# A two-layer decoder trunk on eight cores: the order of an attention slot, bf16 copies of the weights in DRAM, and a logarithm that stays in its PSUM bank

## What is computed (the reference, cut)

```python
for layer in range(2):
    xn = rmsnorm(h, mix_norm_g[layer])
    if layer == 0:
        p = xn @ ab_w_in                      # 1024 -> 2048
        a_out = pool_mixer(a, pool_w, scale)  # trailing means over 2, 4, 8, 16 tokens
        b_out = gate_b * short_conv(gate_c * xb, conv_w, conv_b)
        mix = concat(a_out, b_out) @ ab_w_out
    else:
        p = xn @ cd_w_in                      # 1024 -> 2560
        c_out = spatial_gating(gelu(u), gelu(v), ...)
        d_out = stick_breaking_attention(q, k, v)   # 8 heads of 64, causal
        mix = concat(c_out, d_out) @ cd_w_out
    h = h + mix
    hn = rmsnorm(h, mlp_norm_g[layer])
    h = h + square(relu(hn @ w1)) @ w2        # 1024 -> 4096 -> 1024
return rmsnorm(h, final_norm_g)
# attention: weights = sigmoid(z) * exp(sum over s<j<t of log(1 - sigmoid(z_j)))
```

## Time and profile before

| what | us |
|---|---|
| median of 3 runs | 3147.63 (3145.16 to 3204.56) |
| the profiled execution, device time | 3141.67 |
| its span (first to last instruction, slowest core) | 3140.0 |
| spans of the 8 cores | 3131.6 to 3140.0 |
| TensorE busy | 3028.5 |
| VectorE, ScalarE, GpSimd busy | 1546.5, 1648.8, 928.9 |

### The profile page before, as it was taken

The page is one execution under the profiler, slowest core; times in us unless marked ns, Lnnn a source line. Parts: engine busy times, 40 slices in busy tenths (PEclk is TensorE's granted clock), DMA queues, the critical chain, the costliest instruction groups (busy, mean ns, idle before and its releaser), DMA issues.

```text
span 3140.0 us, 47346 instructions; the slowest of 8 cores (3131.6 to 3140.0 us)
## 1 busy us (share of the span) xinstructions
PE 3028.5 (96%) x14493; PEld 1386.1 (44%) x14493; DVE 1546.5 (49%) x2691; ACT 1648.8 (53%) x3105; POOL 928.9 (30%) x1289
## 2 busy tenths in 40 slices
PE   7999989999989998999999999999999999998998
PEld 3444434444444443444444444444444444443443
DVE  5534556444544447654444664454544464445444
ACT  3312456555466666766664454555666776653212
POOL 5311654111631125411137421144111231115111
PEclk9999999999999999999999999999999999999999
DMA  8455734544754444444456344367343373348543
GB/s 168 68 81 83 167 62 72 73 66 78 150 105 62 63 88 124 82 59 62 62 117 127 58 67 70 61 136 143 56 59 57 65 170 56 57 64 193 78 73 79
DMA packets 159669, 279.46 MB, mean 89 GB/s; under 512 B 16576, under 2 KB 33088, under 8 KB 159424
## 3 DMA queue, kind: packets, MB, share of 16 engines
q0 software_dynamic: 103824, 189.05, 41.2%
q1 hardware_dynamic: 54448, 85.28, 8.8%
q10 hardware_dynamic: 1152, 2.10, 0.2%
HBM read 423.43 MB, written 41.94 MB: 148 GB/s over the span
## 4 chain that ended last, share of the span: by engine, by line
PE 86%; DVE 4%; POOL 3%; DMA 3%; issue 2%; ACT 2%; SPq 1%; DVEq 0%; ACTq 0%; POOLq 0%
PE ps L415 70%; PE ps L961 4%; PE ps L1004 4%; PE ps L989 4%; PE ps L992 3%; POOL acc L525 1%; DMA mix<-mixd 1%; DVE xn L552 1%; DMA mixd<-mix 1%; SPq L469 1%; POOL st L687 0%; PE ps L532 0%; DMA hT<-xT 0%; PE ps L964 0%; POOL wring L394 0%
## 5 line engine op out<-in xcount | busy, mean ns | idle before, releaser
L415 PE MATMUL ps<-xn,wring 128*128 128x512 bf16 x5888 | 1354.0, 381 | 6.7 <-DVE st L666 3.5
L415 PE MATMUL ps<-mix,wring 128*128 128x512 bf16 x5120 | 1166.7, 380 | 14.5 <-DMA mix<-mixd 9.9
L394 POOL DMA_DIRECT2D wring<-wblk x720 | 387.8, 541 | 1712.0 <-PE ps L415 858.8
L415 PEld LDWEIGHTS ps<-xn,wring 128*128 128x128 bf16 x5888 | 574.1, 98 | 681.2 <-issue 26.0
L584 DVE TENSOR_TENSOR hT<-ps,hT 128x512 f32<-128x512 f32 x640 | 442.2, 691 | 705.9 <-PE ps L415 655.5
L415 PEld LDWEIGHTS ps<-mix,wring 128*128 128x128 bf16 x5120 | 499.3, 98 | 601.2 <-issue 20.2
L618 DVE TENSOR_TENSOR mix<-st 128x512 bf16<-128x512 f32 x512 | 358.0, 700 | 612.3 <-ACT st L616 607.7
L616 ACT ACTIVATE st<-ps 128x512 f32<-128x512 f32 x512 | 305.3, 597 | 543.0 <-PE ps L415 538.8
L968 ACT ACTIVATE E<-ps 128x512 f32<-128x512 f32 (+3 forms) x640 | 338.9, 530 | 350.1 <-PE ps L961 194.9
L970 ACT ACTIVATE Lp<-E 128x512 bf16<-128x512 f32 (+3 forms) x640 | 362.0, 566 | 61.6 <-ACT E L968 3.7
L525 POOL TENSOR_TENSOR acc<-acc,sq 128x512 f32<-128x512 f32 x222 | 283.4, 1277 | 290.5 <-ACT sq L519 281.4
(11 more groups left out here) (71 smaller groups left out, 1267.5 us busy)
## 6 DMA issues: line engine op xcount, KB each, us to landing
wring<-wblk POOLq DMA_DIRECT2D x720, 256.0 KB, 5.0
hsp<-hT SPq DMA_DIRECT2D x64, 256.0 KB, 4.2
hT<-hsp SPq DMA_DIRECT2D x64, 256.0 KB, 12.9
hT<-xT SPq DMA_DIRECT2D x56, 256.0 KB, 10.7
oT<-st SPq DMA_DIRECT2D x56, 256.0 KB, 10.8
mix<-mixd SPq DMA_DIRECT2D x8, 1024.0 KB, 9.7
mixd<-mix SPq DMA_DIRECT2D x8, 512.0 KB, 7.1
mixd<-qT SPq DMA_DIRECT2D x32, 128.0 KB, 4.0
```

The source lines that it names most:

```text
L394: (lambda slot, b: (lambda e: e.dma_start(out=self.wring[:, slot, :], in_=self.wblk[b])))(slot, b),
L415: self.S.op("pe", (lambda l, r, i: (lambda pe: pe.matmul(ap, lhsT=l, rhs=r, start=(i == 0), stop=(i == n - 1))))(l, r, i), reads=lts, writ ...
```

## The change

Three parts, independent of one another:

- In `prefetch`, the first use of a block still goes through GpSimd's casting DMA. The block is noted in a list, and the `take` that claims it issues a copy from SyncE's queue, from the ring slot to a new internal DRAM tensor `wbf` of bf16 blocks. The three later uses of each block are plain bf16 loads from `wbf`, issued from SyncE's queue. So there are 180 casting loads, 180 copies and 540 plain loads. A slot's next load also waits for the slot's copy.
- The norm's Ln writes its PSUM bank in place, and Exp reads and writes that bank. The two `ms` tiles go.
- In the attention's `slot`, `st2(n-2)` and `st3(n-3)` are issued ahead of `st1(n)`. The conditions and the stages themselves are as before.

```diff
+        self.wbf = nc.dram_tensor("wbf", [NBLK, 128, 1024], BF16, kind="Internal").ap()
+        self.L_wbf = [None] * NBLK
...
+    def copy_out(self, gb, b, slot):
+        self.S.op("sp", lambda e: e.dma_start(out=self.wbf[b], in_=self.wring[:, slot, :]),
+                  reads=[self.L_ring[slot]], writes=[self.L_wbf[b]], dma_key=("wb", slot))
+
     def prefetch(self, upto=None, after=()):
...
-            self.S.op("pool",
-                      (lambda slot, b: (lambda e: e.dma_start(out=self.wring[:, slot, :], in_=self.wblk[b])))(slot, b),
-                      reads=after, writes=[self.L_ring[slot]], dma_key=("ring", slot))
+            L = self.L_ring[slot]
+            if self.L_wbf[b] is None:
+                self.S.op("pool", (lambda slot, b: (lambda e: e.dma_start(out=self.wring[:, slot, :], in_=self.wblk[b])))(slot, b),
+                          reads=after, writes=[L], dma_key=("ring", slot))
+                self.L_wbf[b] = LT("wbf")
+                self.copies.append((gb, b, slot))
+            else:
+                self.S.op("sp", (lambda slot, b: (lambda e: e.dma_start(out=self.wring[:, slot, :], in_=self.wbf[b])))(slot, b),
+                          reads=[self.L_wbf[b]], writes=[L], dma_key=("hring", slot))
             self.blk_next += 1
...
         assert self.blk_use <= self.blk_next
+        for x in [x for x in self.copies if x[0] < self.blk_use]:
+            self.copies.remove(x)
+            self.copy_out(*x)
         return [(gb + i) % RING for i in range(n)]
...
-            S.op("act", lambda e: e.activation(out=ms[:], in_=nb, func=AF.Ln, scale=1.0 / D, bias=self.cf[:, 60:61]),
-                 reads=[self.L_bank[bi], self.L_cf], writes=[L_ms])
-            S.op("act", lambda e: e.activation(out=nb, in_=ms[:], func=AF.Exp, scale=-0.5),
-                 reads=[L_ms], writes=[self.L_bank[bi]])
+            L_nb = self.L_bank[bi]
+            S.op("act", lambda e: e.activation(out=nb, in_=nb, func=AF.Ln, scale=1.0 / D, bias=self.cf[:, 60:61]),
+                 reads=[L_nb, self.L_cf], writes=[L_nb])
+            S.op("act", lambda e: e.activation(out=nb, in_=nb, func=AF.Exp, scale=-0.5), reads=[L_nb], writes=[L_nb])
...
                 carry(n - 1)
-            if n < N:
-                st1(n)
             if 0 <= n - 2 < N:
                 st2(n - 2)
             if 0 <= n - 3 < N:
                 st3(n - 3)
+            if n < N:
+                st1(n)
```

More of the change, by code:

```diff
@@ L260, in __init__ @@
         self.blk_done = 0
+        self.copies = []
         self.bank_rr = 0
@@ L264, in __init__ @@
         self.nms = 0
-        self.nmt = 0
         self.nvb = 0
@@ L299, in _alloc @@
         self.wmt = sb("wmt", [128, 512], BF16)
-        self.ms = [sb("ms%d" % i, [128, 512], F32) for i in range(2)]
         self.sq = [sb("sq%d" % i, [128, 512], F32) for i in range(2)]
@@ L324, in _alloc @@
         self.L_cf, self.L_cg, self.L_cb, self.L_wmt, self.L_ones = (LT(x) for x in ("cf", "cg", "cb", "wmt", "ones"))
-        self.L_ms = [LT("ms%d" % i) for i in range(2)]
         self.L_sq = [LT("sq%d" % i) for i in range(2)]
@@ L536, in last @@
                 return
-            m = self.nmt % 2
-            self.nmt += 1
-            ms, L_ms = self.ms[m], self.L_ms[m]
-            S.op("act", lambda e: e.activation(out=ms[:], in_=nb, func=AF.Ln, scale=1.0 / D, bias=self.cf[:, 60:61]),
-                 reads=[self.L_bank[bi], self.L_cf], writes=[L_ms])
-            S.op("act", lambda e: e.activation(out=nb, in_=ms[:], func=AF.Exp, scale=-0.5),
-                 reads=[L_ms], writes=[self.L_bank[bi]])
+            L_nb = self.L_bank[bi]
+            S.op("act", lambda e: e.activation(out=nb, in_=nb, func=AF.Ln, scale=1.0 / D, bias=self.cf[:, 60:61]),
+                 reads=[L_nb, self.L_cf], writes=[L_nb])
+            S.op("act", lambda e: e.activation(out=nb, in_=nb, func=AF.Exp, scale=-0.5), reads=[L_nb], writes=[L_nb])
             for k in range(8):
-                self.later(1 + k // rate, (lambda k: (lambda: apply(k, nb, self.L_bank[bi])))(k), key)
+                self.later(1 + k // rate, (lambda k: (lambda: apply(k, nb, L_nb)))(k), key)
         def apply(k, ms, L_ms):
```

## The result

The changed kernel runs in 0.9877 of the time before (95% interval 0.9854 to 0.9899): 38.7 us less of 3146.4. Three of its five executions took 3105.6 to 3107.9 us; in the two others the cores of one die were granted a lower clock, and these, which the median of 3131.8 us on record holds, are left out of the comparison. The profiled execution's span is 3104.1 us against 3140.0. The sign and the range of the prediction held; the forecast of 21 us less was 18 us short, and the gain lies a little outside the 8 to 35 us that it allowed for its own mechanism.

A forecast was written before the change was run, and what follows sets the result against it. TensorE, busy 3028.5 of 3140.0 us, was taken to bound the kernel, leaving 111.5 us idle to win. Terms: 15 + 7 + 9 - 8 - 2 = 21 us won, so a median of 3127 us, range 3098 to 3162.

The forecast's parts named there:

- The slot's order: Attention slot: Exp first on ScalarE, scores last on TensorE, 1.8 us more slack; net 15 us won.
- 23 of the 26 us: Scores matmul L961 waiting for Exp L996: nearly all 24 waits would go; a quarter taken back, 18 us won.
- 3 us worse: Scores now stand behind waits of L1004 and L989: 0.2 us of matmul behind each of 14, 3 us lost.
- GpSimd's relief: 540 loads leave GpSimd, ending stalls mainly at the end of the first p1: 7 us won, bounds 0 and 10.
- 2.6 + 1.7 us here, 1 us at the same place of sequence B: End of first p1: 2.6 us of TensorE waits and 1.7 us of lowered clock won, 1 us in sequence B.
- DMA time: Start of last segment: plain loads shorten the DMA burst, ending the mix tile's wait; 9 us won, bounds -3 and 14.
- keeping 9 against the smaller figure: Last segment: queues served by turns would give some 3 us; 9 kept, as the long burst gave casts their turns.
- The copies at the start: First take: copies queue behind the constants and hold GpSimd's next load some 9 us; 8 us lost, bounds 0 and 15.
- SyncE's order: p1: loads of x stand behind waiting weight loads, some 11 us later but still hidden; 2 us charged.
- more than expected: Rival: short waits form one loop, so L1004's and L989's shrink too and clock stays up; 3107 us, chance 0.10.
- The gain doesn't arrive: Rival: ScalarE itself is short in late windows, so the slot's wait only moves; about 3145 us, chance 0.20.
- slower: Rival: SyncE's one queue; first copy holds GpSimd, weights' waits delay x and h; 3173 us, chance 0.12.

The follow-up runs named there:

- experiment 3: The changed kernel with the 540 plain bf16 loads issued from GpSimd's queue in place of SyncE's; span 3119.5 us, ratio 0.9924 to the kernel before.

## Why the prediction was right or wrong

1. *The slot's order: 15 us forecast, 22.7 measured.* The mechanism held: the Exp of L996 was the last of three and is now the first, and the scores' wait is gone. The size of what it could win was wrong. I took "23 of the 26 us" from the list of waits. That list counts idle time of an engine, and a matmul of 512 columns is shown for 0.38 us while the next one starts 0.216 us after it. So 0.165 us of every wait lies under the modelled end of the matmul before it. In the kernel before, steady part of attention A1:

```profile
1401.03 1.89 PE L415 MATMUL ps<-mix,wring 128*128 128x512 bf16 x8
1402.76 0.38 PE L961 MATMUL ps<-qp,kT 128*128 128x512 bf16 x1
...
1418.86 1.89 PE L415 MATMUL ps<-xn,wring 128*128 128x512 bf16 x8
1420.85 0.38 PE L961 MATMUL ps<-qp,kT 128*128 128x512 bf16 x1
```

From group to scores it is 1.73 us the first time and 1.99 the second: 0.26 us lost, of which the engine looks idle for 0.10. Counted from start to start over the whole trace, the scores behind a dense group lost 45.4 us in 132 waits, not 26.0 in 24. "3 us worse" for the waits of L1004 and L989 was the other wrong size. The same count for every order, each matmul's start against the one before it plus that one's shown time less 0.165 us (medians of the cores whose matmul records are complete):

| kernel, TensorE's order | scores | first suffix sum | Wt times V | freed | span less, measured |
|---|---|---|---|---|---|
| before: scores, sums, Wt times V | 45.7 | 8.6 | 20.5 | | |
| slot's order alone: sums, Wt times V, scores | 2.7 | 10.5 | 35.6 | 26 | 22.7 |
| ScalarE's order alone | 9.1 | 10.7 | 23.2 | 32 | 32.7 |
| changed kernel: sums, Wt times V, scores | 2.7 | 7.8 | 31.7 | | |
| changed, sums, scores, Wt times V | 7.0 | 7.4 | 19.7 | 8 | 7.7 |
| changed, scores, sums, Wt times V | 8.1 | 6.0 | 20.4 | 8 | 10.7 |

So the slot's edit frees 43 us at the scores and gives 15 back at Wt times V and 2 at the sums, where I had 3 us for both. What the count says is freed and what the spans show agree to about 3 us in all four pairs.

2. *GpSimd's relief: 7 us forecast with bounds of 0 and 10, 17.3 measured.* The places were right: the seven loads of rows 6 and the same place of sequence B. The step that failed is "2.6 + 1.7 us here, 1 us at the same place of sequence B". The stall reaches further: the late norm delays the first attention slots behind it, with a wait of L989 for L952 of 2.7 us and another fall of the clock (0.83 and 0.82 from 430 to 440 us in the kernel before, 1.00 at the same place, 435 to 450 us, in the changed one). The runs show 10.5 us for sequence A and 4.9 us for B.

3. *DMA time: 9 us forecast for the last segment, 4 to 6 measured there.* The changed kernel gains 4.2 us on the kernel before from place 2500 to 2525, and 5.7 from place 2500 to the end (medians of the cores). The step that failed is "That removes the 6.56 us [...] with the residual's 4.6 us [...] left as they are": it is the other way round. The waits for h (1.5 to 3.4 us in six of the eight cores before) and the 2.0 us for GpSimd's sum ahead of them are gone: no core of the changed kernel has one over 1.5 us there. TensorE meets the mix tile sooner and waits 6.3 to 9.2 us for it (4.5 to 7.9 before), and the clock still falls, to 0.54 and 0.50. The reason that I gave for keeping 9 against the smaller figure fails with it. By the rule of the Trainium skill ("DMA: Bandwidth & Descriptors", section "SWDGE vs HWDGE vs iDMA") that queues of the two kinds are served by turns, the gain there would have been near 3 us; the traces have 4 to 6, nearer to that than to 9. No run isolates the turns: with the mix tile on the other queue it landed after 13.8 in place of 15.0 us (medians) and the run was 3.6 us shorter. A further 6 us or so came ahead of the last segment change, which I had at nothing; where it arises isn't shown.

4. *The copies at the start: 8 us forecast with bounds of 0 and 15, 12.5 measured (14.4 on the slowest cores).* The chain was as described, to about 1 us: the constants ahead, the first copy late, GpSimd's load waiting 10.15 us (some 9 forecast). The part that failed is that TensorE would feel "about 6 us": it felt all of it, in one wait of 13.4 to 14.5 us on the eight cores, since GpSimd was in the chain of the first mixer with no slack and waited a second time, for slot 1's copy. The granted clock was 0.50 from 50 to 60 us, inside the wait, and 0.64 in the next 5 us.

5. *SyncE's order: 2 us forecast.* Outside the mix tile, TensorE's list for the slowest core has no wait over 1.3 us for x, h or a weight load behind the first x, so the cover held; no run tests the term by itself. The wait of SyncE for casting loads ahead of their copies (316.7 us in 98) is hidden.

6. *The logarithm: 0, measured as no change that can be told.* 24 and 20 ns less per instruction in the run with this edit alone.

The sum by measured terms closes if it is taken along one chain of kernels (before, the slot's order alone, the run of experiment 3, the changed kernel), by the medians of the eight cores: slot 22.4, GpSimd's relief 16.8, bytes 11.8 (the logarithm among them), start -13.3, end of the first p1 -2.1. That is 35.6, of a measured 35.7; such a chain adds up by itself, and each term is good to a few us. So the time fell inside the range in part by luck: the slot and GpSimd's relief were put 7 and 10 us too low, the last segment 4 us too high and the loss at the start 5 us too low. Of the rivals, the time of "more than expected" (3107) is what came, but not its mechanism: L1004's waits grew in place of shrinking. "The gain doesn't arrive" and "slower" each had one true element, the new waits at L1014 and the start.

## What to carry to other kernels

A wait list that goes by idle time undercounts a pipelined engine: compare start to start against the undisturbed interval before a wait is priced. When stages of a software pipeline are reordered, decide the order engine by engine: here the Exp had to come first on ScalarE, while on TensorE the matmul that waits for VectorE had to stay last. A DMA that is put on record as a reader of a buffer, be it a copy of it or only a marker to delay something, holds up the buffer's next load, and at this start, with the DMA engines full (shares of 1.04 to 1.11), the wait was TensorE's from end to end. And compare places in a trace by the medians of the cores: the slowest core of one run can be late by a few us where another run's isn't.

## What was not expected of the hardware

The clock fell only behind some stalls. After the 5 us stretch at 405 us with TensorE busy for 1.99 us (experiment 3) it was 0.50 in the next one, and in and behind the 9.20 us wait in the last segment it was 0.54 and 0.50. Single waits of about 3 us went both ways: in the kernel before, one of 2.66 us at 434 us went with 0.83 and 0.82, while those of 2.98 us at 892, 2.75 at 916 and 2.92 at 1237 left it at 1.00 in the stretches of 5 us around them. The 132 short waits of the scores, 45 us in all, lie mostly in stretches with a mean granted clock of 1.00 (1000 to 1600 and 1800 to 2200 us). And a plain load of 256 KB landed after a median of 2.7 us, against 5.0 us for the casting load of the kernel before (the first three lines are of the changed kernel, the last one of the kernel before):

```profile
wring<-wbf SPq DMA_DIRECT2D x540, 256.0 KB, 2.7
wring<-wblk POOLq DMA_DIRECT2D x180, 256.0 KB, 6.8
wbf<-wring SPq DMA_DIRECT2D x180, 256.0 KB, 6.2
wring<-wblk POOLq DMA_DIRECT2D x720, 256.0 KB, 5.0
```
